# Query norm as a column that scales the scores, key norm made at the key's own RoPE step, in a two-layer sparse attention block

## The reference

```python
q = apply_rope(rms_norm(q.reshape(B, T, N_HEADS_A, HEAD_DIM), qn_g), cos_h, sin_h)
k = apply_rope(rms_norm(k, kn_g), cos, sin)
...
s = jnp.einsum('bqhd,bkd->bqhk', qib.astype(jnp.float32), k_idx_f)
score = jnp.einsum('bqhk,bqh->bqk', jax.nn.relu(s), wib.astype(jnp.float32) * idx_scale)
_, sel = lax.top_k(score, k_top)
...
logits = jnp.einsum('bqhd,bqkd->bqhk', qb, kg).astype(jnp.float32) * attn_scale
p = jax.nn.softmax(logits, axis=-1).astype(vg.dtype)
```

## Time and profile before

| what | before |
|---|---|
| median of 3 runs | 1277.65 us (1276.4 to 1278.24) |
| the profiled execution | 1277.85 us, span 1276.1 us |
| mean granted TensorE clock | 0.994 |
| PE busy | 1247.7 us, 98% of the span |
| PEld busy | 1145.4 us, 90% |
| DVE busy | 622.8 us, 49% |
| ACT busy | 714.4 us, 56% |
| POOL busy | 981.5 us, 77% |
| chain that ended last | PE 92%, DVE 5%, ACT 2% |

### The profile page before, as it was taken

How to read it: one execution, slowest core, us unless ns; L and a number is a source line. 1 busy time by engine, 2 the same in 40 slices (tenths; PEclk the granted TensorE clock), 3 DMA queues, 4 the chain that set the end, 5 groups by cost and what they waited for, 6 DMA issues and landing times.

```text
span 1276.1 us, 22577 instructions
## 1 busy us (share of the span) xinstructions
PE 1247.7 (98%) x8965; PEld 1145.4 (90%) x8965; DVE 622.8 (49%) x1492; ACT 714.4 (56%) x1339; POOL 981.5 (77%) x774
## 2 busy tenths in 40 slices
PE   6999999999999999999999999999999999999997
PEld 5988899988889888889999999999999888888886
DVE  5566755657565444422765566632125234444312
ACT  6454656455565766555654676674447446666532
POOL 4665668766569999989799766768889757899894
PEclk9989999999999999999999999999999999999999
DMA  6543445544346666656466545455656545666662
GB/s 242 144 121 117 133 134 179 150 143 150 106 133 198 183 192 186 187 178 191 146 201 205 150 133 149 135 159 169 181 181 217 157 124 157 190 186 191 174 195 81
DMA packets 57785, 208.92 MB, mean 164 GB/s; under 512 B 6353, under 2 KB 7633, under 8 KB 57425
## 3 DMA queue, kind: packets, MB, share of 16 engines
q1 hardware_dynamic: 57680, 207.48, 54.1%
HBM read 206.41 MB, written 1.05 MB: 163 GB/s over the span
## 4 chain that ended last, share of the span: by engine, by line
PE 92%; DVE 5%; ACT 2%; DMA 0%; issue 0%; POOL 0%; SPq 0%; DVEq 0%
PE bank L386 22%; PE bank L359 17%; PE bank L361 16%; PE bank L360 16%; PE bank L389 11%; PE bank L912 1%; PE bank L701 1%; PE bank L1798 1%; DVE ar L973 1%; PE bank L2175 1%; PE bank L2197 1%; PE bank L2147 1%; PE bank L2149 1%; PE bank L2148 1%; ACT whi L311 1%; PE bank L1782 1%
## 5 line engine op out<-in xcount | busy, mean ns | idle before, releaser
L319 POOL TENSOR_TENSOR wlo<-raw,whi 128x512 fp32r<-128x512 f32 x770 | 981.3, 1304 | 278.9 <-ACT whi L311 277.3
L311 ACT ACTIVATE whi<-raw 128x1024 fp32r<-128x1024 f32 x387 | 404.1, 1052 | 40.9 <-DMA raw<-w_dram 15.6
L359 PE MATMUL bank<-xx,whi 128*128 128x256 f32 (+1 forms) x1296 | 379.3, 293 | 9.8 <-DVE xx L449 9.2
L361 PE MATMUL bank<-xx,wlo 128*128 128x256 f32 (+1 forms) x1296 | 368.6, 284 | 0.0
L360 PE MATMUL bank<-xx,whi 128*128 128x256 f32 (+1 forms) x1296 | 368.2, 284 | 0.0
L359 PEld LDWEIGHTS bank<-xx,whi 128*128 128x128 f32 x1296 | 246.6, 190 | 19.1 <-issue 12.6
L360 PEld LDWEIGHTS bank<-xx,whi 128*128 128x128 f32 x1296 | 246.3, 190 | 0.5
L361 PEld LDWEIGHTS bank<-xx,wlo 128*128 128x128 f32 x1296 | 246.6, 190 | 0.0
L386 PE MATMUL bank<-xx,whi 128*128 128x512 f32 x704 | 178.9, 396 | 0.0
L359 PE MATMUL bank<-yy,whi 128*128 128x256 f32 (+1 forms) x524 | 151.2, 289 | 0.0
L361 PE MATMUL bank<-yy,wlo 128*128 128x256 f32 (+1 forms) x524 | 148.9, 284 | 0.0
(11 more groups left out here) (270 smaller groups left out, 1433.1 us busy)
## 6 DMA issues: line engine op xcount, KB each, us to landing
raw<-w_dram SPq DMA_DIRECT2D x387, 512.0 KB, 3.7
h<-x_dram SPq DMA_DIRECT2D x2, 544.0 KB, 6.2
cst<-con_dram SPq DMA_DIRECT2D x1, 1049.0 KB, 9.8
ar<-mem_dram SPq DMA_DIRECT2D x1, 1024.0 KB, 6.2
out_dram<-h SPq DMA_DIRECT2D x4, 256.0 KB, 2.5
cst<-con_dram SPq DMA_DIRECT2D x1, 134.0 KB, 3.5
prm<-par_dram SPq DMA_DIRECT2D x1, 131.0 KB, 4.4
```

The costliest lines, as they stand in the source:

```text
L311: e.activation(whi[:, i % NSPL, :], raw[:, i % NRAW, :], ACT.Copy).then_inc(*whi_done.done(i))
L319: return e.tensor_tensor(wlo[:, q, c0:c1], raw[:, i % NRAW, c0:c1], whi[:, q, c0:c1].bitcast(F), ALU.subtract)
L359: e.matmul(o, wh, both[:, 0, :], start=(i == 0), stop=False)
L361: m = e.matmul(o, wl, both[:, 0, :], start=False, stop=(i == len(feed) - 1))
```

## The change

The keys' sum of squares gets a bank and a product of its own (64 x 64 ones, so the sum arrives on all 64 partitions). ACT takes its root and DVE the reciprocal and the product right after the key's RoPE. The queries' sums stay in one bank, now of 8 rows; their root (with a bias of 64 eps and no 1/64, which makes it 8 times the RMS) is transposed by PE to one column a head for each tile of 128 tokens. The reciprocal of those columns, `rq`, replaces 0.125 where the scores leave their bank. The five spreading products, the reciprocal of 10 x 272 and the five multiplications of q and k in the u blocks go. The yields of the q norm fall from 5 to 2 on PE and ACT, and from 10 to 4 on DVE, so all that follows in the generator (indexer, meta tokens, attention) comes three blocks earlier. For the meta tokens the two scalings of the scores move from ACT to DVE.

```diff
@@ -649,15 +648,13 @@
             self.q0 = 0 if l == 0 else META
             self.nq = T - self.q0
             (self.qT, self.qiT, self.kT, self.kiT, self.V, self.ga, self.gb, self.mg, self.L, scr0, scr1, pt0, pt1,
-             ra0, ra1, rg0, rg1, ub, tmp0, tmp1, self.m8, self.nm, self.sm, self.rs, self.psh) = arena(
+             ra0, ra1, rg0, rg1, ub, tmp0, tmp1, self.m8, self.nm, self.sm, self.rs, self.psh,
+             self.rq) = arena(
                 (4, T), (4, T), (T,), (T,), (3, 72), (4, T), (4, T), (16, T), (8, T), (T,), (T,), (3, 128), (3, 128),
-                (T,), (T,), (T,), (T,), (16 + T,), (T,), (T,), (8, 8), (8,), (8,), (8,), (4,))
+                (T,), (T,), (T,), (T,), (16 + T,), (T,), (T,), (8, 8), (8,), (8,), (8,), (4,), (3, 8))
             self.scr = [scr0, scr1]
-            self.rr = pt0[0:10, :, :].rearrange("p a b -> p (a b)")[:, 0:T]
             self.ub, self.pw = ub, ra0
-            self.PT = ring(f"PT{l}", [pt0, pt1], 0)
-            self.PT.open(0, (piece, ("qr", l, 3)))
-            self.PT.open(1)
+            self.PT = ring(f"PT{l}", [pt0, pt1])
             self.rope_a, self.rope_g = ring(f"ra{l}", [ra0, ra1]), ring(f"rg{l}", [rg0, rg1])
             self.tmp = ring(f"tmp{l}", [tmp0, tmp1, ra1], 2)
             self.qa = self.L[:, 0:5, :]
@@ -685,10 +682,16 @@
         n = T - c0
         yield
         if kind != "qi":
-            i = 4 if kind == "kk" else b
+            sq = sqb.at("ropesq", l, kind, b)[:, 0:n]
+            if kind == "kk":
+                o = side_.take(e, "kr", l)
+                side_.give(("kr", l), (s_step, ("kroot", l)))
             e.wait_ge(*s_step.of("ropesq", l, kind, b))
-            m = e.matmul(K.ssq[0:10, c0:T], cst[:, C_S10 + 10 * i:C_S10 + 10 * i + 10],
-                         sqb.at("ropesq", l, kind, b)[:, 0:n], start=(kind == "kk"), stop=(i == 3), skip_group_check=True)
+            if kind == "kk":
+                m = e.matmul(o[0:64, 0:n], ones[0:64, 0:64], sq[0:64, :], start=True, stop=True)
+            else:
+                m = e.matmul(K.ssq[0:8, c0:T], cst[:, C_S8 + 8 * b:C_S8 + 8 * b + 8], sq, start=(b == 0), stop=(b == 3),
+                             skip_group_check=True)
             m.then_inc(*piece.done("ropesq", l, kind, b))
         o = side_.take(e, "perm", l, kind, b)[:, 0:n]
         side_.give(("perm", l, kind, b), (v_step, ("sin", l, kind, b)))
@@ -730,6 +733,13 @@
             K.rope_a.give((kind, l, b), (v_step, ("rope", l, kind, b)))
             yield
         yield
+        if kind == "kk":
+            o = K.scr[0][0:64, :]
+            e.wait_ge(*s_step.of("kroot", l))
+            e.reciprocal(o, o).then_inc(*v_step.done("krec", l))
+            e.wait_ge(*v_step.of("krec", l))
+            e.tensor_tensor(K.kT[0:64, :], K.kiT[0:64, :], o, ALU.mult).then_inc(*v_step.done("kT", l))
+            yield
 
     def rope_scalar(e, K, kind, b):
         l, c0 = K.l, (0 if kind == "kk" else K.q0)
@@ -746,6 +756,11 @@
             e.activation(g, x, ACT.Copy, scale=pc(f"kn{l}" if kind == "kk" else f"qn{l}")).then_inc(
                 *s_step.done("ropeg", l, kind, b))
         yield
+        if kind == "kk":
+            e.wait_ge(*piece.of("ropesq", l, "kk", 0))
+            e.activation(K.scr[0][0:64, :], side_.at("kr", l)[0:64, 0:T], ACT.Sqrt, scale=1.0 / 64,
+                         bias=cst[0:64, C_EPS:C_EPS + 1]).then_inc(*s_step.done("kroot", l))
+            yield
 
 
 
@@ -791,52 +806,32 @@
         yield
         yield
         side_.give(("ssq", l), (s_step, ("qroot", l)))
-        for i in (4, 0, 1, 2, 3):
-            c0 = 0 if i == 4 else K.q0
-            o = side_.take(e, "qr", l, i)[:, 0:T - c0]
-            side_.give(("qr", l, i), (v_step, ("qr", l, i)))
-            e.wait_ge(*v_step.of("qrec", l))
-            e.matmul(o, cst[0:10, C_B10 + 128 * i:C_B10 + 128 * i + 128], K.rr[:, c0:T], start=True, stop=True).then_inc(
-                *piece.done("qr", l, i))
-            if i in (0, 2, 3):
-                yield
+        o = side_.take(e, "qc", l)
+        side_.give(("qc", l), (v_step, ("qrec", l)))
+        e.wait_ge(*s_step.of("qroot", l))
+        for i, (t0, n) in enumerate(VALUE_TILES if l == 0 else VALUE_TILES[0:2]):
+            m = e.transpose(o[0:n, 8 * i:8 * i + 8], K.scr[1][0:8, t0:t0 + n], ident[0:8, 0:8])
+        m.then_inc(*piece.done("qc", l))
 
     def qnorm_scalar(e, K):
         l = K.l
+        e.wait_ge(*v_step.of("kT", l))
+        e.activation(K.kT[64:128, :], K.kT[0:64, :], ACT.Copy).then_inc(*s_step.done("k2", l))
+        e.activation(K.kiT[0:64, :], K.kiT[64:128, :], ACT.Copy).then_inc(*s_step.done("ki2", l))
         e.wait_ge(*piece.of("ropesq", l, "q", 3))
-        e.activation(K.scr[1][0:10, 0:T], side_.at("ssq", l)[0:10, 0:T], ACT.Sqrt, scale=1.0 / 64,
-                     bias=cst[0:10, C_EPS:C_EPS + 1]).then_inc(*s_step.done("qroot", l))
-        yield
-        yield
-        for i in (4, 0, 1, 2, 3):
-            if i == 4:
-                e.wait_ge(*v_step.of("qr", l, 4))
-                e.activation(K.kT[64:128, :], K.kT[0:64, :], ACT.Copy).then_inc(*s_step.done("k2", l))
-                e.activation(K.kiT[0:64, :], K.kiT[64:128, :], ACT.Copy).then_inc(*s_step.done("ki2", l))
-            if i in (0, 2, 3):
-                yield
+        e.activation(K.scr[1][0:8, K.q0:T], side_.at("ssq", l)[0:8, K.q0:T], ACT.Sqrt,
+                     bias=cst[0:8, C_EPS64:C_EPS64 + 1]).then_inc(*s_step.done("qroot", l))
+        yield
+        yield
 
     def qnorm_vector(e, K):
-        l = K.l
-        yield
-        e.wait_ge(*s_step.of("qroot", l))
-        e.reciprocal(K.rr, K.scr[1][0:10, 0:T]).then_inc(*v_step.done("qrec", l))
-        yield
-        yield
-        yield
-        for i in (4, 0, 1, 2, 3):
-            c0 = 0 if i == 4 else K.q0
-            o = side_.at("qr", l, i)[:, 0:T - c0]
-            e.wait_ge(*piece.of("qr", l, i))
-            if i == 4:
-                e.wait_ge(*v_step.of("rope", l, "q", 3))
-                e.tensor_tensor(K.kT[0:64, :], K.kiT[0:64, :], o[0:64, :], ALU.mult).then_inc(*v_step.done("qr", l, i))
-            else:
-                x = K.qT[:, i, K.q0:T]
-                e.tensor_tensor(x, x, o, ALU.mult).then_inc(*v_step.done("qr", l, i))
-            if i in (0, 2, 3):
-                yield
-                yield
+        l, o = K.l, side_.at("qc", K.l)
+        for _ in range(4):
+            yield
+        e.wait_ge(*piece.of("qc", l))
+        if l == 0:
+            e.reciprocal(K.rq[0:META, 2, :], o[0:META, 16:24]).then_inc(*v_step.done("mrq", l))
+        e.reciprocal(K.rq[:, 0:2, :], o[:, 0:16].rearrange("p (a b) -> p a b", b=8)).then_inc(*v_step.done("qrec", l))
 
 
 
@@ -924,7 +919,7 @@
             for hh in (2 * s, 2 * s + 1) if s < 4 else ():
                 o, p0 = side_.take(e, "qk", l, t, hh)[:, 0:nk], 64 * (hh % 2)
                 side_.give(("qk", l, t, hh), (v_step, ("qk", l, t, hh)))
-                e.wait_ge(*v_step.of("qr", l, 3))
+                e.wait_ge(*v_step.of("rope", l, "q", 3))
                 e.wait_ge(*s_step.of("k2", l))
                 e.matmul(o, K.qT[p0:p0 + 64, hh // 2, c0:c0 + 128], K.kT[p0:p0 + 64, 0:nk], start=True, stop=True).then_inc(
                     *piece.done("qk", l, t, hh))
@@ -977,8 +972,9 @@
                 e.wait_ge(*v_step.of("sel", l, t))
                 if t:
                     e.wait_ge(*s_out.of("pt", l, 0, hh))
-                e.scalar_tensor_tensor(K.L[:, hh, 0:nk], side_.at("qk", l, t, hh)[:, 0:nk], 0.125, bs, ALU.mult,
-                                       ALU.add).then_inc(*v_step.done("qk", l, t, hh))
+                e.wait_ge(*v_step.of("qrec", l))
+                e.scalar_tensor_tensor(K.L[:, hh, 0:nk], side_.at("qk", l, t, hh)[:, 0:nk], K.rq[:, t, hh:hh + 1], bs,
+                                       ALU.mult, ALU.add).then_inc(*v_step.done("qk", l, t, hh))
             yield
         ob = side_.at("ob", l, t)
         for b in range(4):
@@ -1004,10 +1000,10 @@
     def meta_tensor(e, K):
         l = K.l
         pair = [side_.take(e, "mqk", l, half) for half in range(2)]
-        e.wait_ge(*v_step.of("qr", l, 3))
+        e.wait_ge(*v_step.of("rope", l, "q", 3))
         e.wait_ge(*s_step.of("k2", l))
         for half in range(2):
-            side_.give(("mqk", l, half), (s_out, ("mqk", l, half)))
+            side_.give(("mqk", l, half), (v_step, ("mqk", l, half)))
             for j in range(4):
                 p0 = 64 * half
                 m = e.matmul(pair[half][0:16, 16 * j:16 * j + 16], K.qT[p0:p0 + 64, j, 0:16], K.kT[p0:p0 + 64, 0:16],
@@ -1038,11 +1034,6 @@
     def meta_scalar(e, K):
         l = K.l
         Lm = K.L[0:16, 0, 0:128].rearrange("p (h k) -> p h k", k=16)
-        for half in range(2):
-            e.wait_ge(*piece.of("mqk", l, half))
-            e.activation(Lm[:, 4 * half:4 * half + 4, :],
-                         side_.at("mqk", l, half)[0:16, 0:64].rearrange("p (h k) -> p h k", k=16),
```

(26 more changed lines are left out.)

## The result

| | before | changed |
|---|---|---|
| median (5 runs each) | 1278.24 us | 1284.63 us |
| span of the profiled execution | 1276.1 us | 1282.8 us |
| mean granted clock | 0.994 | 0.990 |

A forecast was written before the change was run, and what follows sets the result against it. PE was taken to set the end. Layer 0 +3.1, layer 1 +0.9 and the key's norm 0.3 made +4.3 us on the profiled 1277.85, 1282.15; median 1282.0 us, range 1273.5 to 1288.

The forecast's parts named there:

- the three blocks: Indexer and meta work enters u blocks already full on DVE, adding PE waits; said to decide; layer 0 +3.1 us.
- The wait behind u1: Layer 0: PE waits 4.5 us before the meta scores, for banks whose accumulations stand behind u1's pooling on DVE.
- The meta scores as the place that decides: Layer 0: a PE wait there of 3.5 to 5.5 us would show the forecast right; under 1.5 us, a faster kernel.
- Part 1: PE work removed in both layers, mainly the spreading products: -5.85 us, -2.8 in layer 0 and -3.05 in layer 1.
- Part 2: Key's reciprocal and product at its RoPE hold DVE 2.3 to 3.3 us; PE loses 0.3 us for both layers together.
- DVE had pauses: Between the RoPE steps, DVE's pauses were to swallow most of the key norm's 2.3 to 3.3 us.
- A PE wait of over 1 us at q0: Listed sign that the forecast is wrong; the delay there was put at 0 to 0.8 us a layer.
- Part 3: Key copies ahead of ACT's query root delay `qrec`; new PE wait 0.9 us in layer 0, 0.75 in layer 1.
- Layer 1: Sum +0.9 us, bounds -3 and +4, including a new PE wait of 2.55 us at the first scores behind gb1.
- the crowded tick: Layer 1: its PE wait, 1.42 us before, moves from mg10 to gb3 and grows by 0.3 us.
- The clock: Low-clock losses behind new waits: 1.8 + 1.0 us in layer 0 against 1.4 before, 0.8 in layer 1.
- Rival (C): Each new wait brings its own low-clock stretch; five long ones of 1.5 us loss give 1285, to 1288; chance 0.10.

The follow-up runs named there:

- e2: Changed kernel with three blocks of yields put back between q norm and indexer, so indexer, meta tokens and attention stand where they stood; 1279.53 us.
- e4: Changed kernel with, in layer 0 alone, the meta tokens' steps and the first attention one block later; 1277.83 us.
- e3: Changed kernel with the key's norm moved behind q1 on DVE, and indexer and attention three blocks later; 1276.04 us.
- e8: e3 with the PE work of the five spreading products put back in layer 0 alone, results unused; 1275.46 us.
- e9: e3 with ACT's rounding of the next weight slot moved behind the copy the scan waits for, in both layers' u blocks; 1273.90 us.
- e1: Changed kernel with the key's reciprocal and product moved on DVE to behind the two ticks of q1; 1280.58 us.
- e6: Changed kernel, key's norm behind q1; layer 0 meta steps and first attention one block later; layer 1 indexer and attention three blocks later; 1271.60 us.

## Why the prediction was right, point by point

- **Slower, because of the three blocks.** Right. Putting them back is worth 5.1 us (e2). The wait behind u1 was to be 4.5 us and is 3.56; the accumulations that it hangs on were to stand behind u1's pooling, and do. That the chain has the length put by hand, 5.95 us from the first accumulation to the meta scores against 5.92 measured (76.50 to 82.42), is partly luck: the first set was put at 1.2 us (75.0 to 76.2) and takes 1.7, as it did before, while scaling and pooling were put at 3.3 us and take 2.58, since the 16-column step met only the end of a POOL instruction here (0.36 us). The drip-fed set fills 2.36 us of the chain, not 1.5. What follows was put at 1.9 and 1.6 us; it is 0.88 and 0.89 + 1.15.
- **The meta scores as the place that decides.** Right. With its low clock I had 6.3 us on it and used the rest of layer 0 to offset that; e4 gets 6.8 us back, of which this wait and its low stretch explain some 4.6.
- **Part 1, PE's 5.85 us.** I took it off in full in both layers. For the forecast that did no visible harm: layer 0 was put at +3.1 us and its share of the key's norm, and came out at +4.50, of which up to 1.5 is the low stretch at 24.5 us; no run puts the work back in the changed order. In the order of before it was wrong, and with it the expectations of e2 and e3. e8 shows that layer 0's 2.9 us were worth nothing there, and e9 why: a loop of 4.24 us was beside it. All the rows needed stood in the trace before: ACT's copies 4.24 us apart. I compared PE's 3.23 us with 3.2 us of DVE busy work, and not with the chain that goes through three engines.
- **Part 2, the key's norm.** The term that was mis-sized most: 0.3 us put, 4.05 us found by e1, of which 0.58 and 1.24 us are PE's waits; that the rest is low clock is argued and not shown. The length was right (1.83 + 0.89 us on DVE where 2.3 to 3.3 was put), but I asked who waits for q0, and the instruction held up was the scaling of the next qi block, standing behind it in the same queue, whose RoPE product PE waits for. "DVE had pauses" was the step that failed: in the qi ticks of both layers it had none. The products and additions there with both inputs in SBUF take 0.7 to 1.4 us beside POOL's subtractions and 0.42 to 0.44 where POOL is idle. A PE wait of over 1 us at q0 had been named as a sign that the prediction is wrong; the 1.24 us in layer 1 are that sign, at qi2.
- **Part 3.** The wait for `qrec` was 0.36 and 0.48 us where 0.9 and 0.75 was put. Right in kind; no experiment touched it alone.
- **Layer 1.** The wait for the first scores was to be 2.55 us and is 2.63; that of the crowded tick grew from 1.42 to 1.76, by the 0.3 put. But the layer came out 3.08 us longer where 0.9 and a share of the key's norm were put. The 2 us between are in the main the key's wait (1.24) and a second low stretch.
- **The clock.** I counted one low stretch over u2, one behind the later waits and one in layer 1. There are two in each layer. The two of before were also read too short: the windows in the earlier trace rows end at 94.90 and 320.30, and the granted clock stays at 0.50 until 95.9 and 321.3. Rival (C), each new wait with its own low stretch, put 1285 for five of them; the profile has five with the one at 24.5 us, and the median is 1284.63. Forecast and (C) differ mainly in this count, and no experiment separates them.

The sum was off by 2.1 us. In the profile both layers are longer than put, layer 0 by about 1.3 us and layer 1 by about 2, and the two causes point the same way: the key's norm and more time at the low clock. The smaller waits, put too long by 2.3 us in all (0.9 + 0.75, 4.5 and 1.9 + 1.6 against 0.36 + 0.48, 3.56 and 0.88 + 0.89 + 1.15), hid a part of both, and that is luck. The kind and place of the loss were foreseen, the middle of the sum was not.

## What to carry to other kernels

Before work is moved, write down for each engine what the moved instruction will stand in front of, not only what it stands behind: a step of 2.7 us costs PE a wait, even on an engine that is busy half of the span, if the engine has no pause in that stage and the step comes before the one instruction that PE's next side product needs. And before PE work is taken off a PE that is 98% busy, look for a loop through the other engines of the same length as PE's block: compare the time from one turn to the next, not busy time. Whether the saving comes back may depend on the order: layer 0 gained nothing in e3 and 3.1 us in e6. Work from a light stage moved into the heavy one gives back what it saved.

## What the runs showed of the hardware that was not expected

A 16-column multiplication on DVE took 1.11 to 1.17 us in each turn of e3 and 0.17 us where POOL was idle (u2 and u3 of the changed kernel). In e3 it starts during POOL's subtraction and ends with it; in u1 of the changed kernel it met only the last 0.34 us of one and took 0.36. The Trainium skill, SBUF — State Buffer, section "SBUF: two separate sides", has an exclusive lock between a DVE instruction with two SBUF inputs and a POOL instruction that reads SBUF; the trace agrees. What was not expected is the regularity: the rounding on ACT that starts the subtraction is itself in the chain, so DVE meets it every turn, and in e9, with the rounding elsewhere in the turn, still each time (1.13 to 1.14 us).

The reciprocal over 272 columns took 1.83 us on 64 partitions in the changed kernel and 1.84 on 10 before, so the columns set its time and not the partitions.

Low stretches of the clock came and went behind equal waits. In e3 PE waits 1.42 us at the crowded tick of layer 1, as long as before, and the stretch behind it runs at full clock, where before it ran at 0.65:

```profile
316.00:319.50 3.50, 3.50 (x28) 3.22 (x30) 0.62 (x3) 0.49 (x1) 2.55 (x2) 1.00 0.31 118
```

What such a stretch costs shows between e3 and e8, whose code in layer 1 is the same: layer 1 takes 165.85 us in e3, without one, and 167.41 in e8, with one from 316.7 to 320.1 us, 1.56 us more in a single execution. That is as much as some of the edits here, and it is why the times above are medians of several.
